# The first feed-forward slot of layer two, computed by token tile with the weights as the moving operand

## The reference

```python
for l in range(2):
    h = _rms_norm(x, norm_mix_pre[l]);  y = _hybrid_mixer(h, ...)
    x = x + _rms_norm(y, norm_mix_post[l])
    h = _rms_norm(x, norm_x_pre[l]);    y = _memory_cross_attention(h, ...)   # ends in o @ w_xo
    x = x + _rms_norm(y, norm_x_post[l])
    h = _rms_norm(x, norm_ffn_pre[l])
    gate, up = jnp.split(h @ w_gu[l], 2, axis=-1)       # 2816 columns each
    y = (jax.nn.silu(gate) * up) @ w_down[l]
    x = x + _rms_norm(y, norm_ffn_post[l])
```

## Time and profile before

| | us |
|---|---|
| runs of the kernel before | 1119.89, 1118.78, 1120.20 (median 1119.89) |
| the profiled execution | 1118.98, its span 1117.2 |
| TensorE busy | 1103.5 (99%) |
| VectorE, ScalarE, GpSimd busy | 563.9, 565.2, 672.3 |

### The profile page before, as it was taken

One profiled execution on the slowest core, in us unless ns is written; L12 is line 12 of the kernel. 1 busy time (PEld: TensorE's weight loads), 2 busy tenths in 40 slices (PEclk: granted clock), 3 DMA queues, 4 the chain that ended last, 5 costly groups with the idle time before them and its releaser, 6 DMA issues.

```text
span 1117.2 us, 20125 instructions
## 1 busy us (share of the span) xinstructions
PE 1103.5 (99%) x8258; PEld 1026.6 (92%) x8258; DVE 563.9 (50%) x1049; ACT 565.2 (51%) x895; POOL 672.3 (60%) x352
## 2 busy tenths in 40 slices
PE   8999999999999999999999999999999999999997
PEld 7999999998898999899999999999978969999996
DVE  6688558455515641234567865593644344212333
ACT  7645854434645544444464567544346545444443
POOL 4866767627673457654477658675378444576442
PEclk9999999999999999999999999999999999999999
DMA  7543444624543655545544434445255254555553
GB/s 286 179 143 133 160 133 161 180 89 151 198 161 124 205 182 187 188 173 187 189 170 170 151 133 152 139 164 157 72 188 190 96 187 152 188 188 181 182 185 114
DMA packets 63339, 183.40 MB, mean 164 GB/s; under 512 B 18576, under 2 KB 19088, under 8 KB 63248
## 3 DMA queue, kind: packets, MB, share of 16 engines
q1 hardware_dynamic: 47936, 172.48, 44.1%
q10 hardware_dynamic: 15312, 9.64, 3.3%
HBM read 179.47 MB, written 2.62 MB: 163 GB/s over the span
## 4 chain that ended last, share of the span: by engine, by line
PE 95%; DMA 2%; ACT 1%; DVE 1%; issue 1%; POOL 0%; SPq 0%; ACTq 0%; DVEq 0%; POOLq 0%
PE psum L484 27%; PE psum L485 27%; PE psum L486 26%; DMA sb_raw<-weights 2%; PE psum L632 1%; PE psum L959 1%; PE psum L938 1%; PE psum L676 1%; PE psum L659 1%; PE psum L562 1%; PE psum L853 1%; PE psum L846 1%; PE psum L643 1%; PE psum L728 1%; ACT sb_high L373 0%
## 5 line engine op out<-in xcount | busy, mean ns | idle before, releaser
L383 POOL TENSOR_TENSOR sb_low<-sb_raw,sb_high 128x1024 fp32r<-128x1024 f32 x258 | 620.8, 2418 | 350.7 <-ACT sb_high L373 336.0
L373 ACT ACTIVATE sb_high<-sb_raw 128x1024 fp32r<-128x1024 f32 x322 | 340.4, 1061 | 430.0 <-DMA sb_raw<-weights 378.7
L484 PE MATMUL psum<-sb_h_high,sb_high 128*128 128x256 f32 x1664 | 471.6, 283 | 0.7 <-DVE sb_low L383 0.7
L486 PE MATMUL psum<-sb_h_high,sb_low 128*128 128x256 f32 x1664 | 469.6, 282 | 0.0
L485 PE MATMUL psum<-sb_h_low,sb_high 128*128 128x256 f32 x1664 | 469.5, 282 | 0.0
L484 PEld LDWEIGHTS psum<-sb_h_high,sb_high 128*128 128x128 f32 x1664 | 314.6, 189 | 3.0 <-issue 1.1
L485 PEld LDWEIGHTS psum<-sb_h_low,sb_high 128*128 128x128 f32 x1664 | 313.0, 188 | 0.9
L486 PEld LDWEIGHTS psum<-sb_h_high,sb_low 128*128 128x128 f32 x1664 | 312.7, 188 | 0.0
L383 DVE TENSOR_TENSOR sb_low<-sb_raw,sb_high 128x1024 fp32r<-128x1024 f32 x64 | 101.7, 1596 | 38.3 <-ACT sb_high L373 37.8
L2046 DVE SCALAR_TENSOR_TENSOR sb_sq<-sb_th,psum 128x512 f32<-128x512 f32 x22 | 15.1, 688 | 148.4 <-ACT sb_th L1462 148.4
L1806 DVE SCALAR_TENSOR_TENSOR sb_conv<-psum,sb_param,sb_conv 128x255 f32<-128x255 f32 (+1 forms) x144 | 58.3, 474 | 46.7 <-ACT sb_conv L1262 46.7
(11 more groups left out here) (280 smaller groups left out, 1529.5 us busy)
## 6 DMA issues: line engine op xcount, KB each, us to landing
sb_raw<-weights SPq DMA_DIRECT2D x322, 512.0 KB, 3.2
sb_pre_gain<-pre_gains ACTq DMA_DIRECT2D x6, 512.0 KB, 4.4
sb_post_gain<-post_gains ACTq DMA_DIRECT2D x6, 512.0 KB, 4.2
sb_kx<-mem SPq DMA_DIRECT2D x2, 512.0 KB, 4.3
sb_x<-x SPq DMA_DIRECT2D x1, 1024.0 KB, 10.8
t_dram<-sb_sq ACTq DMA_DIRECT2D x4, 256.0 KB, 2.9
out<-sb_x SPq DMA_DIRECT2D x4, 256.0 KB, 2.1
m_dram<-sb_m ACTq DMA_DIRECT2D x8, 64.0 KB, 2.0
```

The source lines that it names most:

```text
L373: nc.scalar.activation(high[:, n % HIGHS, :], raw[:, n % RAWS, :], ACT.Copy).then_inc(high_ready, 1)
L383: eng.tensor_tensor(low[:, k, :], raw[:, k, :], high[:, n % HIGHS, :].bitcast(F32), ALU.subtract).then_inc(low_ready[k], 1)
L484: pe.matmul(out, a[0], b[0], start=start, stop=False, **kw)
L486: return pe.matmul(out, a[1], b[0], start=False, stop=stop, **kw)
```

## The change

It concerns layer two only (`layer + 1 == DEPTH`); layer one is as before.

- The cross output's steps i = 2 and 3 are done by tile: all four halves for tile 0, then all four for tile 1 (`two_by_tile`). PE's mark for tile 0 and the releases of the four halves move with it.
- ScalarE, GpSimd and VectorE get the norm work in another order (`norms_by_tile` on ScalarE and on VectorE, `between` on GpSimd and VectorE): the squares, root, normed tile of tile 0 come before the residual of tile 1, with one weight half's high or low part between the steps.
- Slot 0 of the feed-forward (`first_slot`): h is stationary, 256 weight columns are moving, the result is token by feature. PE does the transposes of tile 0, two bf16 matmuls of `keep_busy`, most of the products of tile 0, the transposes of tile 1, and the products of tile 1. The products are issued in groups of four matmuls.
- Slot 0's gated product is written to SBUF (`ff_tok`), PE turns it with four transposes after gate 1 (`ff_transposes`), and the high and low parts for the down product are taken from there.
- VectorE subtracts all four halves of slot 0's weights.
- On the host these four halves are laid out as 512 rows by 256 columns in place of 1024 rows by 128.

```diff
+            if layer + 1 == DEPTH and part in ("gate", "up") and i == 0:
+                return True                      # vector_low
...
+                def two_by_tile(part, act, outs):
+                    w = []
+                    for c in range(TILES):
+                        for i in (2, 3):
+                            for b in range(2):
+                                if c == 0:
+                                    w.append(weights_here(HALF_AT[layer, part, i, b]))
+                                for k2 in range(2):
+                                    k = 4 * (i % 2) + 2 * b + k2
+                                    mm = product(outs[c], pick(act, lambda t: t[:, k, c * P:(c + 1) * P]),
+                                                 pick(w[2 * (i - 2) + b], lambda t: t[:, k2 * 512:(k2 + 1) * 512]), k == 0, k == KT - 1)
+                                if c == 1:
+                                    mm.then_inc(slots.sem, mark(slots, (part, i) if b else ((part, i), "first")))
                         if c == 0:
                             mm.then_inc(pe_out.sem, mark(pe_out, part))
...
+                def first_slot():
...
+                    def four(key, c, b, of_h, of_w):
+                        for k4 in range(4):
+                            k = 4 * b + k4
+                            mm = pe.matmul(gate_up[key][:, c * 256:(c + 1) * 256], h[of_h][:, k, c * P:(c + 1) * P],
+                                           w[key, b][of_w][:, k4 * 256:(k4 + 1) * 256], ...)
...
+                    turned(0)
+                    keep_busy(2, 1)
...
+                    for b in range(2):
+                        high_here("gate", b)
+                        pe.wait_ge(*act_part.at(layer, ("h", "ffn", 0, b)))
+                        four("gate", 0, b, 0, 0)
+                        weights_here(HALF_AT[layer, "gate", 0, b])
+                        four("gate", 0, b, 0, 1)
+                    high_here("up", 0)
+                    four("up", 0, 0, 0, 0)
+                    for b in range(2):
+                        pe.wait_ge(*dve_part.at(layer, ("h_low", "ffn", 0, b)))
+                        four("gate", 0, b, 1, 0)
+                    four("up", 0, 0, 1, 0)
+                    high_here("up", 1)
+                    four("up", 0, 1, 0, 0)
+                    four("up", 0, 1, 1, 0)
+                    weights_here(HALF_AT[layer, "up", 0, 0])
+                    four("up", 0, 0, 0, 1)
+                    turned(1)
+                    weights_here(HALF_AT[layer, "up", 0, 1])
+                    four("up", 0, 1, 0, 1)
...
+                def norms_by_tile():                                   # ScalarE
+                    half_squares("x", "xo")
+                    act.wait_ge(*pe_out.at(layer, "xo"))
+                    last_square("x", 0)
+                    high_parts(ahead("xo", 0))
+                    for half in range(2):
+                        act.wait_ge(*dve_norm.at(layer, ("x", "x", 0, half)))
+                        square_x("ffn", 0, half)
+                    high_parts(ahead("xo", 1))
+                    act.wait_ge(*slots.at(layer, ("xo", 3)))
+                    last_square("x", 1)
+                    for half in range(2):
+                        h_high("ffn", 0, half)
+                    high_parts(ahead("xo", 2))
...
-                post_and_pre_norm("x", "xo", 2, "ffn")
+                    norms_by_tile()
...
-                    high_parts(ahead(("gate", i), 3))
+                    high_parts(ahead(("gate", i), 1 if i == 0 and layer + 1 == DEPTH else 3))
...
-                    postnorm("x", "xo", 1)                             # VectorE
-                    prenorm("ffn", 2)
+                    postnorm("x", "xo", 1, between=norms_by_tile)      # between the tiles: low gate 0, normed tile 0, low gate 1
+                    h_low("ffn", 0)
+                    low_parts(ahead("xo", 3))
+                    norm_tile("ffn", 1)
+                    low_parts(ahead("xo", 4))
+                    h_low("ffn", 1)
...
+                    if turned:
+                        low_parts(ahead(("up", 0), 4))
```

More of the change, by code:

```diff
@@ L1011, in _ @@
                     next_keys(1)
-                else:
-                    norm_transposes("ffn")
                 def down(i):
@@ new lines, in ff_transposes @@
+                def ff_transposes():
+                    what = ("ff_t", 0)
+                    pe.wait_ge(*dve_ff.at(layer, ("ff", 0)))
+                    o = claim(what, (dve_part, ("ff_low", 0)), range(4))
+                    for k in range(2):
+                        for c in range(TILES):
+                            tr = pe.transpose(o[:, k * S + c * P:k * S + (c + 1) * P], ff_tok[:, c * 256 + k * P:c * 256 + (k + 1) * P], ident)
+                    tr.then_inc(pe_t.sem, mark(pe_t, what))
@@ L1063, in _ @@
                         wide(("gate", i), h, (dve_ff, ("silu", i)), range(4))
-                    wide(("up", i), h, (dve_part, ("ff_low", i)), range(4))
+                    if i == 1 and by_tile:
+                        ff_transposes()
+                    if i > 0 or not by_tile:
+                        wide(("up", i), h, (dve_part, ("ff_low", i)), range(4))
                     if i == 0:
@@ L1497, in rsqrt, with prenorm @@
                     nc.gpsimd.tensor_tensor(r, r, neghalf[:, 0:1], ALU.pow).then_inc(pool_norm.sem, pool_norm.mark(name))
-                def prenorm(which, more=None):
-                    for c in range(TILES):
+                def prenorm(which, more=None, tiles=range(TILES)):
+                    for c in tiles:
                         if more is not None:
@@ L1506, in prenorm, with postnorm @@
                         rsqrt(ss[:, c:c + 1], rs[:, c:c + 1], act_norm, ("ss", which, c), ("pre", which, c), more_x[:, c:c + 1])
-                def postnorm(part, product):
+                def postnorm(part, product, between=None):
                     if product != "down":
@@ L1516, in postnorm @@
                     for c in range(TILES):
+                        if between and c == 1:
+                            between()
                         if product == "down":
@@ L1522, in postnorm @@
                         else:
-                            low_parts(ahead(product, 1 if part == "x" else 2))
+                            low_parts(ahead(product, 1 if part == "x" else 2) - (HIGHS - 3 if between else 0))
                         pool.wait_ge(*pool_norm.at(layer, ("half", part, c)))
@@ L1651, in prenorm, with postnorm @@
                                             h[0][:, to[0], to[1]].bitcast(F32), ALU.subtract).then_inc(dve_part.sem, dve_part.mark(("h_low", which, c, half)))
-                def postnorm(part, product, row, final=False):
+                def postnorm(part, product, row, final=False, between=None):
                     start = 512
@@ L1666, in postnorm @@
                             scale_first(c)
-                        low_parts(ahead(product, 2))
+                        low_parts(ahead(product, 0 if between else 2))
                     else:
@@ L2039, in _ @@
                         mem_lows(half, KT * (2 * layer + 2))
-                postnorm("x", "xo", 1)
-                prenorm("ffn", 2)
+                if layer + 1 < DEPTH:
+                    postnorm("x", "xo", 1)
+                    prenorm("ffn", 2)
+                else:
+                    postnorm("x", "xo", 1, between=norms_by_tile)
[4 more added lines that the diff above has]
+                    h_low("ffn", 1)
                 for i in range(FF_SLOTS):
-                    low_parts(ahead(("gate", i), 2 if i else 3))
+                    turned = i == 0 and layer + 1 == DEPTH
+                    low_parts(ahead(("gate", i), 2 if i or turned else 3))
                     dve.wait_ge(*act_ff.at(layer, ("tanh", i)))
@@ L2120, in lay_out @@
                 to[:] = blocks(part("v")[512 * b:512 * (b + 1)]).reshape(P, HALF)
+            elif name in ("gate", "up") and i == 0 and layer + 1 == DEPTH:
+                to[:] = blocks(mats[name][512 * b:512 * (b + 1), 0:256]).reshape(P, HALF)
             elif name == "down":
```

109 lines of the change are left out of this document (100 added, 9 removed).

## The result

The changed kernel takes 1122.20 us (median of 20 runs, 1120.13 to 1124.59) against 1119.74 (20 runs, 1118.33 to 1121.35): ratio 1.0024, 95% interval 1.0018 to 1.0030. It is 2.5 us slower where 2.0 us of gain were forecast, and outside the range. Its profiled execution took 1121.98 us, its span is 1120.2.

A forecast was written before the change was run, and what follows sets the result against it. TensorE, busy 99% of the span, was taken as the bound; 7.64 us without gate or up products would become 5.6 of waits, transposes and fillers, gaining 2.0 us: median 1117.9, range 1116.3 to 1120.9.

The forecast's parts named there:

- The stall in the cross output: Cross output by tile needs weights at twice the pace; TensorE waits 0.6 us for the fourth half's low part.
- the pace of the moving side: Slot 0's 96 products with h stationary and weights moving keep their pace: cost 0, between −0.1 and +0.2 us.
- the raw weights: Cross output releases four weight halves later; gate's second half arrives at 914.5, up's at 915.9 and 917.3.
- VectorE as the pacemaker from 915 to 925: VectorE runs norm, residual and low parts back to back, 9.5 to 9.8 us, the last done at 924.7.
- gate 1's low part: At the start of slot 1, TensorE waits 0.5 us for GpSimd's low part of gate 1's first half.
- the turning back: Four transposes of slot 0's token-major product after gate 1, with the handover 0.5 us; the product's readiness is hidden.
- Slot 1: Second feed-forward slot: gate 1's weights, released late, are ready at 931.4, so TensorE waits 0.5 us.
- the end of slot 0: Gate and up of slot 0 end at 931.0, against 934.1 in the kernel before.
- rival C: Clock falls to 1.2 GHz from 916 to 925 for lack of fillers: +5 us, median 1123; chance 0.05.
- B: Rival: late-released weight halves make TensorE wait repeatedly in slot 1; gain 0 to 1.3 us, median 1119.2; chance 0.20.
- A: Rival: VectorE's chain closes up and TensorE's waits shrink; gain 2.7 to 3.4 us, median 1116.8; chance 0.18.
- D: Rival: late DMAs delay tile 1's norm work on ScalarE, which becomes pacemaker; a smaller loss, 1120.5 to 1122.5; chance 0.07.

The follow-up runs named there:

- experiment 6: Changed kernel with gate 1 in PSUM bank 2 and two low parts moved (one earlier on VectorE, one from GpSimd to VectorE): 1116.66 us against 1118.98 before.
- experiment 5: Changed kernel with gate 1 given PSUM bank 2 by name, so it does not wait for silu: 1117.98 us against 1118.98 before (0.9992).
- experiment 9: experiment 6 without the two fillers between tile 0's transposes and its first products: 1117.44 us against 1119.24 before (0.9979).
- experiment 1: Changed kernel with an edit meant to move gate 1 to bank 2 that had no effect, so a repeat: 1122.12 us against 1118.84 before.
- experiment 4: Changed kernel, the ineffective bank edit, and gate 1's first-half low part on VectorE instead of GpSimd: 1122.53 us, ratio 1.0038 to the kernel before.
- experiment 3: Changed kernel, bank kept, with slot 0's tanh and silu ahead of gate 1's second-half high and low parts: 1118.45 us against 1118.84 before.
- experiment 10: experiment 6 with the low part of slot 0's second up half on GpSimd instead of VectorE: 1118.48 us against 1119.24 before (0.9995).
- experiment 8: Kernel before the change without its 12 fillers behind the cross output: 1120.78 us against 1118.98 with them (1.0017).
- experiment 2: Changed kernel with 14 fillers on TensorE between slot 0 and gate 1: 1120.84 us against 1118.84 before (1.0019).

## Why the prediction was wrong

*What held.* The stall in the cross output (0.6 forecast, 0.5 found; gone in experiment 6), the pace of the moving side, the raw weights, VectorE as the pacemaker from 915 to 925 (its last low part 0.5 us later than worked out), gate 1's low part (0.5 forecast, 0.57 and 0.58 once the bank was free) and the turning back (0.5 forecast; 12.02 us from gate 1 to down in experiment 5, 11.52 before) are as the steps said. With the bank free, experiment 5 gains 1.0 us by the medians and 1.37 in its profile (from cross output to down 892.32 to 944.49 = 52.17 us), inside the range and short of the 2.0 mostly by the smaller miss below. In the step on VectorE the working says eight groups of four matmuls between h's low part and up's last low part; the program has six, and the 924.3 that the working gives fits six.

*The step that failed* is "Slot 1": "PE waits 0.5 us", for its weights; in the sum, the term 0.5 (gate 1 low), which measured 3.38 us from the end of slot 0 to gate 1, 3.23 of it idle. I listed what gate 1's weights need and not what gate 1's matmuls wait for besides. The sum also had no term for the clock, which was put at 1.00 on the ground that no forecast gap was over 0.7 us; it took 1.4 us more. The working itself held the number: by it the product is ready at about 935, so silu, the step before it, not much sooner, and gate 1 starts at 931.5. What links the two is the bank, and that is not a line of the change: `claim` gives gate 1 bank 0 in both kernels. Before, gate 0 ended 5.8 us ahead of up 0, and silu ran under up 0. The change brings gate 0 and up 0 to within 2.8 us of each other (tile 1's gate, then tile 1's up). Tanh stands in both kernels behind a high part whose DMA starts only when slot 0 releases its first half, and that release now comes 3.1 us before the end of the slot in place of 8.45. A wait with 3.0 us of slack became one of 3.2 us.

*The clock* (rival C, 0.05) came about, by another way than that rival's. C looked at 915 to 930, where the clock stayed at 1.00 with transposes, two fillers and gaps of 0.5 us; experiment 9 shows it at 1.00 without the two fillers. It fell behind the wait that was not foreseen, in two of the three profiled executions with that wait. The mean clock of each whole execution says more: of the 30 executions with the wait (the changed kernel, experiments 1 and 4), 22 show 0.997 or less, and only three 1.000, which are the fastest of their kernels (1120.13, 1120.89, 1121.11). None of the 77 of the kernel before that ran beside experiments 1 to 10 shows 0.997 or less, nor any of the 22 of experiments 3 and 5. The changed kernel spreads over 4.5 us in 20 runs against 3.0 before; that this comes from the clock is not shown, as experiment 8 has the fall without a wider spread. C's price was read from the fillers at the start of the kernel; the profile gives a granted clock of 1.00 for 1.50 to 5.00 us there, so that those were slow by the clock is not shown.

The Trainium skill ("TensorE: Matmul & The Clock Gate", Part 4, PE-mode transpose) has it that transposes do not count as activity in the same way. The stretch at risk by that rule, from 915.76 to 917.86, held no fall in any of the profiles with the changed order and short gaps; the falls all follow an idle of 1.8 us or more. Experiment 10 leaves the rule open: behind its idle of 1.82 us the clock was 1.00 over the eight transposes (925.60 to 926.70) and fell in the products behind them.

*The smaller miss* is the end of slot 0, 0.5 us late. By the rows it comes from GpSimd's tiny steps, which I took from rows in which VectorE was at other work; no run tests it. Beside VectorE's low part the root's power takes 1.56 us in place of 0.55, and the first addition 1.01 in place of 0.19. The addition ends at 914.69, just behind the low part that began before it at 913.42 and ended at 914.64:

```profile
913.68 1.01 POOL L1646 TENSOR_TENSOR sb_tiny<-sb_tiny,sb_const 128x1 f32<-128x1 f32 x1 [1.69 <-ACT sb_region_a L1209]
...
915.03 0.55 POOL L1639 TENSOR_TENSOR sb_tiny<-sb_tiny,sb_const 128x1 f32<-128x1 f32 x1
...
920.40 0.19 POOL L1646 TENSOR_TENSOR sb_tiny<-sb_tiny,sb_const 128x1 f32<-128x1 f32 x1 [1.83 <-ACT sb_region_a L1209]
...
921.39 1.56 POOL L1639 TENSOR_TENSOR sb_tiny<-sb_tiny,sb_const 128x1 f32<-128x1 f32 x1
```

VectorE's prenorms wait for these. Tile 0's starts 0.2 to 0.3 us late, and 0.44 us of idle time stand ahead of tile 1's, where the forecast had it back to back.

```profile
913.42 1.22 DVE L384 TENSOR_TENSOR sb_low<-sb_raw,sb_high 128x1024 fp32r<-128x1024 f32 x1
915.62 1.41 DVE L1784 SCALAR_TENSOR_TENSOR sb_region_a<-sb_x,sb_tiny,sb_pre_gain 128x512 f32<-128x512 f32 x2 [0.98 <-POOL sb_tiny L1639]
...
921.33 1.22 DVE L384 TENSOR_TENSOR sb_low<-sb_raw,sb_high 128x1024 fp32r<-128x1024 f32 x1
922.99 1.42 DVE L1784 SCALAR_TENSOR_TENSOR sb_region_a<-sb_x,sb_tiny,sb_pre_gain 128x512 f32<-128x512 f32 x2 [0.44 <-POOL sb_tiny L1639]
```

*The account*: −2.1 forecast (its steps put down at 943.5; its sum says 943.6 and 2.0), +0.5 (end of slot 0), +2.9 (the bank), +1.4 (the clock) = +2.7, against +2.64 in the profiles and +2.5 in the medians.

*Rivals.* B is ruled out as the cause: with the bank free (experiments 3 and 5) one wait of 0.6 us is left in slot 1, with the halves released as late as in the changed kernel. A did not occur. D's place was right in one point, a high part that waits for its DMA holds up ScalarE's queue, but behind it stood tanh, not the norm.

## What to carry to other kernels

For every product that starts earlier or whose operands come earlier, list all it waits for, the release of its output buffer too: a reuse with slack before is a dependence that the change can put on the path, although no line of the diff touches it. Where two results that were made one after the other are made to end closer together, whatever ran between them (here tanh and silu) is on the path. And in an in-order queue, a copy that waits for a DMA goes behind the step that frees a buffer, not ahead of it, where the time between the release and the next use is short (experiment 3).

An idle time of TensorE is to be priced with what the clock may take behind it: here taking a wait from 3.3 us to 0.6 gave 3.7 (experiment 1 against experiment 3).

## What the runs showed of the hardware

- A fall of the granted clock to 0.50 (means of 0.50 to 0.66 over windows of 3.0 to 5.2 us) follows some idle times of TensorE and not others of the same length: after 3.26 us none (experiment 1), after 3.23, 3.27, 3.31 and 3.96 a fall, after 1.82 a fall (experiment 10), after 1.51 none. The length alone doesn't decide, and what does stays open. One fall cost 1.4 us and one 2.6 in rows of equal work (13.40 and 14.60 us against 12.0). Fillers in the gap kept it at 1.00 (experiment 2, and the kernel before against experiment 8: 1.8 us).
- When VectorE and GpSimd ran instructions with two operands in SBUF at once, the one that began second stood until the first was nearly done or done, and the first kept its pace. In experiment 10 GpSimd's subtraction began first and kept 2.37 us, while VectorE's two prenorm instructions went from 1.42 to 3.52. In the changed kernel VectorE's low parts began first and kept 1.22, while GpSimd's one-column steps went from 0.19 to 1.01 and from 0.55 to 1.56. In the kernel before, VectorE's 2.65 us from 926.03 ended 1.1 us behind the end of GpSimd's first low part (2.40 from 925.19). Beside VectorE's low part of h, which reads one operand from PSUM, the one-column addition kept its 0.19 (at 920.40). The Trainium skill ("GPSIMD Engine Reference", Specifications, the row on SBUF interfaces) says that the two share their interfaces and contend when a VectorE instruction has two SBUF inputs; the traces agree, with these numbers.
